# Last-row squares summed in PSUM by TensorE, three rows of U moved behind the last evacuation, and V weighted on GpSimd in a two-layer mixing and FFN kernel

## The reference

```python
u = _modulate(_rms_norm(h, g_pre_mix[l]), sm, cm)          # latent and context tokens
y = _mixing(u_lat, u_ctx, ...)                             # attention | retention | pooling | convolution, then w_out
h = h + gm * _rms_norm(y, g_post_mix[l])
f = _swiglu(_modulate(_rms_norm(h, g_pre_ffn[l]), sf, cf), w_ffn_gate[l], w_ffn_up[l], w_ffn_down[l])
h = h + gf * _rms_norm(f, g_post_ffn[l])
```

## Time and profile before

| | |
|---|---|
| median of 3 runs | 3274.9 us (3274.47 to 3276.96) |
| the profiled execution | 3276.1 us, its span 3274.0 us |
| granted TensorE clock, mean over the span | 0.944 |
| busy share of the span | TensorE 88%, VectorE 61%, ScalarE 37%, GpSimd 19% |
| chain that ended last | TensorE 61%, issue 18%, VectorE 12%, ScalarE 5%, GpSimd 2% |

### The profile page before, as it was taken

How to read it: one execution, slowest core, us unless ns; L and a number is a source line. 1 busy time by engine, 2 the same in 40 slices (tenths; PEclk the granted TensorE clock), 3 DMA queues, 4 the chain that set the end, 5 groups by cost and what they waited for, 6 DMA issues and landing times.

```text
span 3274.0 us, 46686 instructions
## 1 busy us (share of the span) xinstructions
PE 2883.8 (88%) x17578; PEld 1603.1 (49%) x17578; DVE 1996.9 (61%) x2744; ACT 1204.8 (37%) x2076; POOL 608.8 (19%) x456
## 2 busy tenths in 40 slices
PE   4799896878999999999997579896789899999997
PEld 3455562554545656757754234463554344444443
DVE  5894687884366414636645695578883664274765
ACT  5111325775444212313324311326773443231332
POOL 0500021000225302202212230011001243120311
PEclk8899996999999999999998789998999999999998
DMA  5111111221134321111141221212222242112133
GB/s 207 55 40 38 36 43 42 89 82 58 60 124 135 121 77 46 49 42 44 48 147 34 96 71 39 49 41 81 101 101 71 93 139 83 45 52 64 52 130 115
DMA packets 69312, 248.90 MB, mean 76 GB/s; under 512 B 9248, under 2 KB 10016, under 8 KB 69152
## 3 DMA queue, kind: packets, MB, share of 16 engines
q1 hardware_dynamic: 68000, 241.44, 22.0%
q10 hardware_dynamic: 1152, 5.24, 0.4%
HBM read 221.75 MB, written 19.92 MB: 74 GB/s over the span
## 4 chain that ended last, share of the span: by engine, by line
PE 61%; issue 18%; DVE 12%; ACT 5%; POOL 2%; DMA 1%; SPq 0%; DVEq 0%; POOLq 0%; ACTq 0%
PE PS L777 36%; PE PS L882 17%; DVE R L2139 4%; DVE wlo L1801 2%; PE PS L1178 2%; ACT X L1430 1%; ACT R L1428 1%; DVE R L1963 1%; DVE R L1950 1%; ACT whi L1313 1%; POOL R L2541 1%; DMA R<-in_w_ada 1%; PE PS L1102 1%; PE PS L1201 1%; PE PS L811 1%
## 5 line engine op out<-in xcount | busy, mean ns | idle before, releaser
L777 PE MATMUL PS<-R,whi 128*128 128x512 f16 (+1 forms) x5216 | 1428.6, 361 | 98.8 <-DVE wlo L1801 57.4
L777 PE MATMUL PS<-R,wlo 128*128 128x512 f16 (+1 forms) x2608 | 940.5, 361 | 0.0
L777 PEld LDWEIGHTS PS<-R,whi 128*128 128x128 f16 x5216 | 509.5, 99 | 633.6 <-issue 72.5
L882 PE MATMUL PS<-R,whi 128*128 128x256 f16 (+2 forms) x2352 | 510.3, 326 | 0.0
L1801 DVE SCALAR_TENSOR_TENSOR wlo<-stage,whi 128x1024 f16<-128x1024 f32 (+1 forms) x204 | 278.6, 1366 | 364.6 <-ACT whi L1313 363.7
L777 PEld LDWEIGHTS PS<-R,wlo 128*128 128x128 f16 x2608 | 257.9, 99 | 256.6 <-issue 14.9
L882 PE MATMUL PS<-R,wlo 128*128 128x256 f16 (+2 forms) x1176 | 319.1, 326 | 0.0
L882 PEld LDWEIGHTS PS<-R,whi 128*128 128x128 f16 x2352 | 230.1, 98 | 152.0
L1313 ACT ACTIVATE whi<-stage 128x1024 f16<-128x1024 f32 (+1 forms) x204 | 210.4, 1031 | 140.4 <-PE PS L777 85.0
L2139 DVE SCALAR_TENSOR_TENSOR R<-X,small,R 128x1024 f32<-128x1024 f32 (+1 forms) x180 | 218.9, 1263 | 1.8
L2468 POOL TENSOR_TENSOR X<-X 128x512 f32<-128x512 f32 (+1 forms) x98 | 135.5, 1386 | 453.7 <-ACT X L1705 331.9
(11 more groups left out here) (219 smaller groups left out, 3468.8 us busy)
## 6 DMA issues: line engine op xcount, KB each, us to landing
stage<-in_w_gu SPq DMA_DIRECT2D x120, 512.0 KB, 3.8
X<-in_w_ada SPq DMA_DIRECT2D x60, 512.0 KB, 3.3
stage<-in_w_down SPq DMA_DIRECT2D x48, 512.0 KB, 3.4
stage<-in_w_in SPq DMA_DIRECT2D x44, 512.0 KB, 3.3
stage<-in_w_out SPq DMA_DIRECT2D x32, 512.0 KB, 3.3
h_save<-R SPq DMA_DIRECT2D x24, 640.0 KB, 5.3
R<-h_save SPq DMA_DIRECT2D x24, 640.0 KB, 4.6
T<-in_w_ada SPq DMA_DIRECT2D x20, 512.0 KB, 3.6
```

Of the source, the lines that this page charges most:

```text
L777: last = mm(slot(into, t0, t1)[:, c0 - t0:c1 - t0], w[:, j, k, :], row, start=(k == 0 and q == 0), stop=(k == K - 1 and q == 2))
L882: last = mm(s_bank(nf, t, o, n), w[:, j, k0 + k, :], row, start=(k == 0 and x == 0), stop=(k == PAIRS - 1 and x == 2))
```

## The change

It has three parts.

1. *Sums in PSUM.* For the steps at the end of a layer (the last Y step of both layers, and in layer 0 the H step behind it) `per_token` is replaced by `end_sums`. For the Y step GpSimd still adds rows 1 to 6 into row 0; TensorE sums that over partitions, and then adds the square of row 7 to the same PSUM columns. For the H step TensorE takes all 8 squares one after another, accumulating in PSUM, and GpSimd adds none. TensorE now signals that a square's buffer is free. The semaphore `sumsq` is no longer counted in these steps, and VectorE's `inverse_root` is split into `mean_square` and `diagonal`, with the same instructions.
2. *Rows of U.* In layer 0 `END_SLOTS` has rows (0, 1, 2) at unit 6 and (3, 4) at unit 7; rows 5, 6 and 7 come behind the last evacuation, on VectorE around the mean and the diagonal of the Y step, on ScalarE ahead of the spread's copy.
3. *V for forward states.* The weighting L2225 goes from VectorE to GpSimd, with a semaphore `vw_fwd` for which TensorE waits in addition.

```diff
+        END_SLOTS = dict(OUT_SLOTS[0], u=((),) * 6 + ((0, 1, 2), (3, 4)))
...
+            def end_sums(k):
+
+                inst, a0, a1 = STEPS[k]
+                ready, used, n = ("y_sq_ready", "y_sq_used", Y_STEPS.index(STEPS[k])) if inst % 2 else \
+                    ("h_sq_ready", "h_sq_used", H_STEPS.index(STEPS[k]))
+                rows = (0, KD - 1) if inst % 2 else range(KD)
+                for d in rows:
+                    if inst % 2 and d == 0:
+                        pe.wait_ge(S[used], (KD - 1) * n + KD - 2)
+                    else:
+                        pe.wait_ge(S[ready], KD * n + d + 1)
+                    src = xrow(2 + d % 2 if d else 0)
+                    for x in range((a1 - a0) // P):
+                        last = mm(PS[:, 7, x:x + 1], src[:, a0 + x * P:a0 + (x + 1) * P], ones[:, 0:1],
+                                  start=(d == 0 and x == 0), stop=(d == KD - 1 and x == (a1 - a0) // P - 1))
+                    if d:
+                        last.then_inc(S[used], 1)
...
                 def products(i):
                     pe.wait_ge(S["vw"], at("vw", l) + i + 1)
+                    pe.wait_ge(S["vw_fwd"], at("vw_fwd", l) + i + 1)
...
-                        norm_hook(i, OUT_SLOTS[0] if l < LAYERS - 1 else LAST_SLOTS, step_of(4 * l + 3, 0))
+                        norm_hook(i, END_SLOTS if l < LAYERS - 1 else LAST_SLOTS, step_of(4 * l + 3, 0))
+                k = step_of(4 * l + 3, 1)
+                end_sums(k)
                 pe.wait_ge(S["slot_free"], unit0(l + 1, "in"))
-                k = step_of(4 * l + 3, 1)
-                per_token(k)
                 spread(k)
                 if l < LAYERS - 1:
-                    per_token(k + 1)
+                    end_sums(k + 1)
                     spread(k + 1)
...
@@ ScalarE
                 k = step_of(4 * l + 3, 1)
+                if l < LAYERS - 1:
+                    for d in (5, 6, 7):
+                        modulated(k3 + 1, d)
                 spread_out(k)
...
@@ VectorE, weighted(i)
-                    TT(heads(T[:, 512 + c:768 + c]), heads(vtok[:, t, :]), by_head(8, 1), ALU.mult)
-                    TT(heads(vw_fwd[:, c:c + 256]), heads(vtok[:, t, :]), by_head(8, 0), ALU.mult).then_inc(S["vw"], 1)
+                    TT(heads(T[:, 512 + c:768 + c]), heads(vtok[:, t, :]), by_head(8, 1), ALU.mult).then_inc(S["vw"], 1)
...
                 k = step_of(4 * l + 3, 1)
-                inverse_root(k)
+                if l < LAYERS - 1:
+                    for d in (5, 6):
+                        scale_row(k3 + 1, d)
+                        low_row(k3 + 1, d - 2)
+                    mean_square(k)
+                    scale_row(k3 + 1, 7)
+                    low_row(k3 + 1, 5)
+                    diagonal(k)
+                    low_row(k3 + 1, 6)
+                    low_row(k3 + 1, 7)
+                else:
+                    inverse_root(k)
                 add_rows(k, Y, range(KD))
...
@@ GpSimd
+                pool.wait_ge(S["pw_ps"], at("pw_ps", l) + 2 * len(spans(t0)))
+                for i in range(NTILE):
+                    pool.wait_ge(S["v_tok"], at("v_tok", l) + i + 1)
+                    if i >= 2:
+                        pool.wait_ge(S["kv_ps"], at("kv_ps", l) + i - 1)
+                    TT(heads(vw_fwd[:, (i % 2) * 256:(i % 2) * 256 + 256]), heads(vtok[:, B_ORDER[i], :]), by_head(8, 0),
+                       ALU.mult).then_inc(S["vw_fwd"], 1)
...
-                    add_square(k, i)
+                    if i < KD - 1:
+                        add_square(k, i)
                 root(k)
                 if l < LAYERS - 1:
-                    for d in range(KD):
-                        add_square(k + 1, d)
                     root(k + 1)
```

More of the change, by code:

```diff
@@ L91, in step_of, with end_steps, sums_made @@
         2 if (inst, half) != (0, 0) and inst and inst < 4 * LAYERS - 1 else 1)
+def end_steps():
+    return [step_of(4 * l + 3, 1) + x for l in range(LAYERS) for x in range(2 if l < LAYERS - 1 else 1)]
+def sums_made(k):
+    return sum(x not in end_steps() for x in range(k + 1))
 def rows_before(inst, half):
@@ L245, in build @@
             b_tab=32, gate_tanh=4, roped_ps=12, roped=12, d_tab=16,
-            states_zero=1, tr_ps=NTILE, v_tok=NTILE, k_tok=NTILE, vw=NTILE, kv_ps=NTILE, state=NTILE - 1, kv_fwd=NTILE - 1,
+            states_zero=1, tr_ps=NTILE, v_tok=NTILE, k_tok=NTILE, vw=NTILE, vw_fwd=NTILE, kv_ps=NTILE, state=NTILE - 1, kv_fwd=NTILE - 1,
             state_fwd=NTILE - 1,
@@ L453, in build, with by_head @@
         block = ctx.enter_context(nc.Block())
+        def by_head(col0, half):
+            return rtab[:, col0 + 4 * half:col0 + 4 * half + 4].rearrange("p (h e) -> p h e", e=1).to_broadcast([P, HB, 64])
+        heads = lambda ap: ap.rearrange("p (h e) -> p h e", h=HB)
         B_ORDER = [1, 0] + list(range(NTILE - 1, CT - 1, -1))
@@ L1778, in _ @@
                             if half:
-                                norm_slot(i, OUT_SLOTS[0] if l < LAYERS - 1 else LAST_SLOTS, k3)
+                                norm_slot(i, END_SLOTS if l < LAYERS - 1 else LAST_SLOTS, k3)
                             act.wait_ge(S["slot_free"], u + 1)
@@ L1897, in units, with mean_square, diagonal @@
                 pairs(dve, n, body)
-            def inverse_root(k):
+            def mean_square(k):
                 inst, a0, a1 = STEPS[k]
                 n = (a1 - a0) // P
-                dve.wait_ge(S["sumsq"], k + 1)
+                if k not in end_steps():
+                    dve.wait_ge(S["sumsq"], sums_made(k))
+                elif inst % 2:
+                    dve.wait_ge(S["y_sq_used"], (KD - 1) * (Y_STEPS.index(STEPS[k]) + 1))
+                else:
+                    dve.wait_ge(S["h_sq_used"], (KD - 1) * (H_STEPS.index(STEPS[k]) + 1))
                 TS(per_tok[:, 0, 0:n], PS[:, 7, 0:n], 1.0 / D, 1e-6, ALU.mult, ALU.add).then_inc(S["mean_sq"], 1)
+            def diagonal(k):
+                inst, a0, a1 = STEPS[k]
+                n = (a1 - a0) // P
                 dve.wait_ge(S["root"], k + 1)
@@ L1912, in inverse_root @@
                    ALU.mult).then_inc(S["diag"], 1)
+            def inverse_root(k):
+                mean_square(k)
+                diagonal(k)
             def scale_row(k, d):
@@ L2209, in _ @@
                 lo_part(u0 + 19, 1, KD)
-                def by_head(col0, half):
-                    return rtab[:, col0 + 4 * half:col0 + 4 * half + 4].rearrange("p (h e) -> p h e", e=1).to_broadcast([P, HB, 64])
-                heads = lambda ap: ap.rearrange("p (h e) -> p h e", h=HB)
                 def weighted(i):
@@ L2440, in _ @@
                                     dve.wait_ge(S["h_back"], 16 * KD * (2 * l + 2))
-                                norm_slot(i, OUT_SLOTS[0] if l < LAYERS - 1 else LAST_SLOTS, k3, Y)
+                                norm_slot(i, END_SLOTS if l < LAYERS - 1 else LAST_SLOTS, k3, Y)
                             dve.wait_ge(S["units"], u + 1)
```

## The result

The changed kernel takes 3251.1 us (median of 4 runs, 3248.4 to 3255.7), the kernel before 3274.7 (4 runs, 3273.8 to 3277.0). The ratio is 0.9929 (95%: 0.9916 to 0.9942), 23.5 us less (by the interval 19.0 to 27.5), where 18.4 was forecast; the forecast time was 3256.5, between 3248 and 3264. The profiled execution of the changed kernel is the slowest of its four: 3255.7 us, span 3253.9, clock 0.949.

A forecast was written before the change was run, and what follows sets the result against it. TensorE, busy for 88% of the span, bounds the kernel; the change shortens its waits. 12.7 + 1.4 + 4.3 = 18.4 us off the profiled 3276.1 gives 3257.7, as a median 3256.5, range 3248 to 3264.

The forecast's parts named there:

- Last evacuation: End of layer 0: the evacuation behind the last down unit starts at 1781.5 and not at 1790.25.
- Sum of Y: End of layer 0: row 7's six products take 2.0 us, between 1.5 and 2.7; the sum ends 10.3 us earlier.
- Rows of U: End of layer 0: rows 5 to 7, moved behind the evacuation, are covered by other waits, with 1.7 us margin.
- H sums: Layer 0's H step: TensorE takes every square at clock 0.50, 2.72 us a row; stretch 25.7 us, 2.4 less.
- Layer 1's end: End of layer 1: GpSimd's add (1.26 us) and a gap of 0.14 go, 1.4 us less.
- V on GpSimd: V and K products: without one weighing VectorE's round falls from 2.0 to 1.65 us; 2.2 less per layer, 4.3 in both.
- 7 if TensorE also keeps its fast clock: V and K products: they save 7 us instead of 4.3 if the fast clock lasts into the next stage.
- The sum: Whole kernel: 12.7 at layer 0's end, 1.4 at layer 1's and 4.3 in the products make 18.4 us less.
- The clock rising in the H sums: Layer 0's H step: VectorE sets the pace, stretch 17.7 us instead of 25.7, kernel 3248.5; chance 0.1.
- GpSimd and VectorE meeting in every round: V and K products: a round takes up to 2.3 us, +5 instead of -4.3, kernel up to 3266; chance 0.16.
- A drain at each hand-over: Layer 0's H sums: a row costs twice the burst price, 5.4 us, stretch 47, kernel 3278; chance 0.03.
- That the wait isn't shortened: End of layer 0: the 10.3 us is only 2 or 3, with GpSimd and VectorE meeting too; kernel 3270 or so; chance 0.05.

The follow-up runs named there:

- no_v: The changed kernel with V for the forward states weighted on VectorE again, all else kept: 3260.6 us, ratio 0.9944.
- only_v: The kernel before with only V for the forward states weighted on GpSimd: 3268.3 us, ratio 0.9978.
- v_twice: The changed kernel with GpSimd's V product done twice in each round, same result: 3259.8 us, ratio 0.9954.
- warm_ahead: The changed kernel with 12 idle 512-column products on TensorE ahead of the H sums: 3250.5 us, ratio 0.9923.
- row_sums: The changed kernel with the H sums made with ones stationary and the squares moving: 3247.5 us, ratio 0.9913; run again 3249.3, 0.9924.
- warm_all: The changed kernel with idle wide products between rows of H squares, ahead of the H sums and ahead of each spread: 3254.6 us, ratio 0.9936.

## Why the prediction was right, point by point

**Last evacuation.** Forecast to start 8.75 earlier, measured 8.77 (9.69 - 0.92). The square's end, 2.95 behind the evacuation's start by the forecast's times, is at 2.97.

**Sum of Y.** Taken as 2.0 between the bounds 1.5 and 2.7; it is 1.60, at the fast clock. At the same time a gap that was called unchanged grew: the mean to the first H row takes 6.87, before 6.43. GpSimd's root, 1.33 elsewhere, takes 1.71 there beside the low row of U that VectorE now makes (1783.82). Both misses are 0.4 and cancel, by luck: 10.25 against 10.3.

**Rows of U.** Covered, as said. VectorE's last moved row ends at 1788.07, 1.9 ahead of the first H row.

**H sums.** Mechanism right, at the slow clock without a pause; the price is the mis-sized term. 2.72 was the length of one burst of 12 records with its tail. In a stream the tail counts once: 20.64 / 8 = 2.58 a row. The stream on record had said so, since 20 records in 4.43 are 2.66 for 12, tail included. The stretch is 3.8 shorter and not 2.4. The relief for VectorE was worth nothing here, as forecast: it runs ahead and TensorE ends the stretch.

**Layer 1's end.** 1.4 forecast, 1.4 measured.

**V on GpSimd.** 2.2 per layer forecast, 2.21 measured; GpSimd's product is 0.61 where 0.67 was taken from a sum of that size, and it meets VectorE in the first weightings, hardly afterwards. Against VectorE's 0.42 it is 1.45 times as long, and the 0.67 was 1.6 times: slower, but neither is the factor of two with which the forecast called it in agreement. The step that failed is the one behind it: TensorE's clock into the next stage stood only in the range ("7 if TensorE also keeps its fast clock") and was left out of the sum. It keeps it, in both layers, for 3.2; `no_v` and `only_v` show that it hangs on this part. All eleven traces with rounds of 1.66 keep the clock in both layers; of the three traces with rounds of 1.95 to 1.99 (the kernel before, `no_v`, `v_twice`) it fell in five of six layers. Why it falls there is open: shorter pauses of TensorE in the rounds are one reading, but `v_twice`, whose rounds are nearly as long as before, fell in one layer and held in the other.

**The sum.** 18.4 forecast; 1.4 more in the H sums and 3.2 behind the rounds make 23.0, where the places give 23.1 and the runs 23.5. The forecast of the time was 5.4 too high (3256.5 against 3251.1).

**The rivals.** The clock rising in the H sums is refuted for this stream: 0.50 through 20.64 us without a pause, and a fall to 0.50 even from 1.00 in warm_ahead. With the same squares in 512- and 256-column products the clock did rise, in `row_sums`. The Trainium skill ("TensorE: Matmul & The Clock Gate", Part 1: The HAM clock gate) says that sustained activity releases the throttle. The traces agree for `row_sums` and for the wide products of `warm_all` ahead of its spreads, and not for the one-column stream, where TensorE is busy for 4.00 of 4.00 us and the clock stays at 0.50. GpSimd and VectorE meeting in every round is refuted for the change and was produced by v_twice. Here the Trainium skill ("GPSIMD Engine Reference", 8. Key points) says that GpSimd shares its SBUF interfaces with VectorE and contends with instructions of two SBUF inputs; the trace agrees, 0.74 and 0.83 against 0.42 for the weighting, 2.55 against 1.01 for the H row. A drain at each hand-over is refuted by the unbroken 96 records. That the wait isn't shortened is refuted by the 12.45.

## What to carry to other kernels

Price a stream of short instructions by the stream: the length of one burst holds a tail that is paid once. When the engine beside TensorE that bounds a pipeline gets faster, look at the granted clock in the stage behind it, since the change can be worth nearly as much again there (3.2 beside 4.4). For a sum over partitions that TensorE can't hide, make the data the moving operand with 512 columns rather than the stationary one with a single column: it took 1.7 instead of 2.58 a row here, because the clock rises; at 0.50 it would have gained nothing. The trace shows the gain in both runs; the total time doesn't show it clear of the noise.

## What the runs showed of the hardware

- One-column f32 products, two records each, took 0.43 (2.58 / 6) at a clock of 0.50 and 0.25 (1.50 / 6) at 1.00. Unbroken for 20.64 us they didn't raise the clock, and where 12 wide products had kept it at 1.00 up to their first row they didn't hold it; two 512-column products between every 12 records didn't either: in one run the second row was slow again, in the other, with a shorter pause ahead and 18 wide products, the third.
- Products with 512 and 256 moving columns raised it in the middle of their stretch, with the same squares, the same waits and fewer records (32 against 96).
- Work meant to raise the clock runs at the slow price until it does: 12 wide products took 4.33 and 5.07 where the clock rose only near their end, and 3.10 where it rose in their first microsecond, as it also does at that place without them. It was seen to rise, and to stay at 1.00 for 3.2, while TensorE stood behind 2.90 of f32 products with 512 and 256 columns.
- GpSimd's two-input product over 128x256 f32 took 0.61, VectorE's 0.42: 1.45 times as long. A VectorE instruction with two SBUF inputs that met it grew to 0.74 and 0.83.
- The clock fell for 3.4 us behind the old rounds of 2.0, in both layers of two kernels, behind rounds of 1.95 in one layer of two, and behind none of the rounds of 1.66 (22 layers in eleven traces), with the same products in each round.
